# The taps of a depthwise convolution moved from VectorE to ScalarE and POOL, in a fused two-block kernel

## The reference, cut to what matters

```
y_a = gdn_mixer(...)     # gated delta rule: per chunk a triangular matrix is inverted, then a state runs over chunks
y_b = dsa_mixer(...)     # indexed attention: keys by top-128 of index scores, then softmax over them
y_c = conv_mixer(ug, dw, dw_b, ln_g, ln_b)
x = x + concatenate([y_a, y_b, y_c]) @ w_out

def conv_mixer(ug, dw, dw_b, ln_g, ln_b):
    u, gate = split(ug, 2)
    y = u * sigmoid(gate)
    y = causal_depthwise_conv(y, dw) + dw_b        # 31 taps, 256 channels
    y = layer_norm(y, ln_g, ln_b)                  # mean and variance over the 256 channels
    return silu(y)
```

## Time and profile before

| what | value |
|---|---|
| median of 3 runs | 1610.46 us (1610.21 to 1611.06) |
| profiled execution, its own time | 1610.98 us |
| its span, first to last instruction | 1609.2 us |
| granted TensorE clock | 0.996 of full |
| PE busy in the span | 98% |
| DVE busy in the span | 57% |
| ACT busy in the span | 43% |
| POOL busy in the span | 10%, all of it in the first fifth |

### The profile page before, as it was taken

One profiled execution on the slowest core, in us unless ns is written; L12 is line 12 of the kernel. 1 busy time (PEld: TensorE's weight loads), 2 busy tenths in 40 slices (PEclk: granted clock), 3 DMA queues, 4 the chain that ended last, 5 costly groups with the idle time before them and its releaser, 6 DMA issues.

```text
span 1609.2 us, 21520 instructions
## 1 busy us (share of the span) xinstructions
PE 1573.3 (98%) x7488; PEld 1305.9 (81%) x7488; DVE 918.1 (57%) x1322; ACT 685.1 (43%) x997; POOL 157.9 (10%) x97
## 2 busy tenths in 40 slices
PE   5999999999999999999999999999999999999997
PEld 5788798888788888888788888888888888888886
DVE  5469799765664324444477666666455544544332
ACT  5635554554653213433245455554224434443221
POOL 2435586200000000000000000000000000000000
PEclk9999999999999999999999999999999999999998
DMA  7422100122132232323233333333222323222332
GB/s 278 164 89 69 53 1 1 66 92 92 40 103 93 92 104 92 100 96 104 59 109 104 94 94 94 94 94 107 102 92 92 105 91 104 91 96 85 100 98 78
DMA packets 45665, 149.50 MB, mean 93 GB/s; under 512 B 4784, under 2 KB 5936, under 8 KB 45616
## 3 DMA queue, kind: packets, MB, share of 16 engines
q1 hardware_dynamic: 42240, 139.90, 27.2%
q10 hardware_dynamic: 3376, 8.95, 1.5%
HBM read 146.47 MB, written 2.10 MB: 92 GB/s over the span
## 4 chain that ended last, share of the span: by engine, by line
PE 90%; DVE 6%; ACT 2%; DMA 2%; issue 0%; ACTq 0%; DVEq 0%; SPq 0%
PE acc L628 84%; DVE c_acc L2109 1%; DVE tok L2249 1%; DMA x<-xT 1%; DVE d_score_a L2252 1%; DVE d_score_b L2252 1%; DMA raw<-panels_a 0%; PE acc L1114 0%; PE acc L1135 0%; DVE g_x L2235 0%; DVE w_lo L1977 0%; PE acc L801 0%; PE acc L703 0%; ACT w_hi L1378 0%; PE acc L939 0%
## 5 line engine op out<-in xcount | busy, mean ns | idle before, releaser
L628 PE MATMUL acc<-h_hi,w_hi 128*128 128x512 f32 x1248 | 491.5, 394 | 1.4 <-issue 0.8
L628 PE MATMUL acc<-h_lo,w_hi 128*128 128x512 f32 x1248 | 486.6, 390 | 0.0
L628 PE MATMUL acc<-h_hi,w_lo 128*128 128x512 f32 x1248 | 486.5, 390 | 0.0
L1985 DVE TENSOR_TENSOR w_lo<-raw,w_hi 128x1024 fp32r<-128x1024 f32 (+2 forms) x241 | 281.6, 1171 | 79.7 <-ACT w_hi L1385 57.6
L1385 ACT ACTIVATE w_hi<-raw 128x1024 fp32r<-128x1024 f32 (+2 forms) x241 | 242.0, 1008 | 175.5 <-PE acc L628 87.1
L628 PEld LDWEIGHTS acc<-h_hi,w_hi 128*128 128x128 f32 x1248 | 234.9, 188 | 52.4 <-issue 3.8
L628 PEld LDWEIGHTS acc<-h_hi,w_lo 128*128 128x128 f32 x1248 | 234.7, 188 | 49.1
L628 PEld LDWEIGHTS acc<-h_lo,w_hi 128*128 128x128 f32 x1248 | 234.8, 188 | 48.1 <-issue 1.0
L2390 DVE TENSOR_TENSOR x<-x,acc 128x512 f32 x32 | 22.0, 688 | 136.5 <-PE acc L628 136.0
L628 PE MATMUL acc<-u_hi,w_hi 128*128 128x512 f32 x256 | 99.6, 389 | 0.0
L628 PE MATMUL acc<-u_lo,w_hi 128*128 128x512 f32 x256 | 99.6, 389 | 0.0
(11 more groups left out here) (400 smaller groups left out, 2316.2 us busy)
## 6 DMA issues: line engine op xcount, KB each, us to landing
raw<-panels_a SPq DMA_DIRECT2D x112, 512.0 KB, 3.2
raw<-panels_b SPq DMA_DIRECT2D x68, 512.0 KB, 3.2
raw<-mix SPq DMA_DIRECT2D x48, 448.0 KB, 3.3
raw<-mix SPq DMA_DIRECT2D x16, 512.0 KB, 3.6
raw<-down SPq DMA_DIRECT2D x16, 384.0 KB, 3.1
raw<-down SPq DMA_DIRECT2D x16, 320.0 KB, 2.9
x<-xT ACTq DMA_DIRECT2D x4, 1024.0 KB, 9.8
x_rows<-xN ACTq DMA_DIRECT2D x2, 1024.0 KB, 9.6
```

The lines of the kernel that those rows point to most:

```text
L628: mm = e.matmul(out, w[:, w_at:w_at + wn], a, start=first and n == 0, stop=last and n == 2)
L1985: TTn(lo, raw, k.w_hi[:, ahead.slot(w)].bitcast(F32), ALU.subtract).then_inc(k.s_split_done, 1)
```

## The change

All 31 taps of tile 0 and the last 12 of tile 1 are now made by ScalarE and POOL: 43 parts in place of 31. One part lies in each of the 24 units, and the last seven are two to a pair in pairs 0 to 3; POOL has 24 adds in the units and nine behind. VectorE keeps the 19 taps ahead of the inverse. Selection is no longer two rounds in three units but four steps in every unit, 96 in all as before. The mean moves from behind unit 21 to pair 5, its subtraction from behind unit 22 to pair 6, the sums of squares from pair 1 to pairs 10 and 11 (in bank 0), the variance to pair 12. outputs(4), the first to use bank 3 again, waits for the subtraction. POOL's squares and its split of panels 32 to 34 stand behind all adds, thus behind pair 6. The turned probabilities d_pt move from the memory of c_y to that of g_p.

```diff
--- before.py
+++ after.py
@@ -48,6 +48,8 @@
 DOWN_W = [(b - a) * P for a, b in zip(DOWN_CUTS, DOWN_CUTS[1:])]
 MIX_GATES = next(p for p in range(8) if 34 <= MIX_CUTS[p + 1])
 CONV_TAPS = 31
+DVE_TAPS = 19
+CONV_PARTS = 2 * CONV_TAPS - DVE_TAPS
 PAD = 32
 
 REST, CKV, CQ, UG, Z = 0, 1, 2, 4, 8
@@ -121,7 +123,7 @@
     "xk_sq d_gates_tok beta_done sp_exp xk_std dec_exp k_root dk_raw d_std go_std aq_std ").split())}
 
 DVE_ONCE = {n: i + 1 for i, n in enumerate((
-    "sp_in xk_inv g_ready dec_copied br qe dv_done d_inv dk_done c_dve c_bias go_bias go_inv "
+    "sp_in xk_inv g_ready dec_copied br qe dv_done d_inv dk_done c_bias go_bias go_inv "
     "aq_inv ").split())}
 
 
@@ -199,6 +201,7 @@
     k.sq, sq_end = sb("sq", 2 * T)
     k.g_sq, _ = sb("g_sq", 2 * T, at=sq_end - 2 * T * 4)
     k.g_p, _ = sb("g_p", 2 * T, at=sq_end - 2 * T * 4)
+    k.d_pt, _ = sb("d_pt", 2 * T, at=sq_end - 2 * T * 4)
     k.tok, _ = sb("tok", NTOK)
     top[0] += (128 - top[0]) % 512
     h0 = top[0]
@@ -224,7 +227,6 @@
     k.d_q, a = sb("d_q", 2 * T, at=a)
     k.d_k, a = sb("d_k", T, at=a)
     k.d_score_b, a = sb("d_score_b", T, at=a)
-    k.d_pt, _ = sb("d_pt", 2 * T, at=a)
     k.c_y, a = sb("c_y", 2 * (PAD + T), at=a)
     k.c_acc, a = sb("c_acc", 2 * T, at=a)
     k.c_t, _ = sb("c_t", 2 * T, at=a)
@@ -341,6 +343,7 @@
     k.s_c_y = sem("c_y")
     k.s_c_part = sem("c_part")
     k.s_c_pool = sem("c_pool")
+    k.s_c_dve = sem("c_dve")
     k.s_c_cent = sem("c_cent")
     k.s_c_sq = sem("c_sq")
     k.s_c_norm = sem("c_norm")
@@ -567,15 +570,16 @@
         TTn(til(k.g_b, u % 4).rearrange("p (c i) -> p c i", c=TT), til(k.g_at, h).rearrange("p (c i) -> p c i", c=TT),
             mask, ALU.mult).then_inc(k.s_bt_done, 1)
 
-    acc = k.c_acc[:, 0:T]
-
     def conv_add(n):
 
         e.wait_ge(k.s_c_part, n + 1)
         if n:
             e.wait_ge(k.s_c_pool, n)
-        other = acc if n else col(k, "dw_b").broadcast_to([P, T])
-        TTn(acc, til(k.c_m, n % 2), other, ALU.add).then_inc(k.s_c_pool, 1)
+        if n == CONV_TAPS:
+            e.wait_ge(k.s_c_dve, DVE_TAPS)
+        sums = til(k.c_acc, int(n >= CONV_TAPS))
+        other = sums if n else col(k, "dw_b").broadcast_to([P, T])
+        TTn(sums, til(k.c_m, n % 2), other, ALU.add).then_inc(k.s_c_pool, 1)
 
     first = FRONT_AT["q0"] + SPLIT + 1
     early = 8 + len(FRONT_AT)
@@ -585,8 +589,9 @@
             conv_add(p - first)
     for u in range(UNITS):
         masked(u)
-        if early - first + u < CONV_TAPS:
-            conv_add(early - first + u)
+        conv_add(early - first + u)
+    for n in range(early - first + UNITS, CONV_PARTS):
+        conv_add(n)
     for j in range(2):
         e.wait_ge(k.s_c_cent, j + 1)
         TTn(til(k.c_t, j), til(k.c_acc, j), til(k.c_acc, j), ALU.mult).then_inc(k.s_c_sq, 1)
@@ -912,23 +917,25 @@
         mm.then_inc(k.s_xp_mm, 1)
         if 1 <= u <= UNITS - HEADS:
             turn_inverse(u - 1)
-        if u == UNITS - 3:
-
-            e.wait_ge(k.s_c_pool, CONV_TAPS)
-            e.wait_ge(k.s_dve_once, DVE_ONCE["c_dve"])
-            for j in range(2):
-                mm = e.matmul(k.ps[3][:], ones, til(k.c_acc, j), start=j == 0, stop=j == 1)
-            mm.then_inc(k.s_pe_once, 1)
     left("z3")
     left("kt3")
-    def centred_squares():
+
+    def conv_mean():
+
+        e.wait_ge(k.s_c_pool, CONV_PARTS)
+        for j in range(2):
+            mm = e.matmul(k.ps[3][:], ones, til(k.c_acc, j), start=j == 0, stop=j == 1)
+        mm.then_inc(k.s_pe_once, 1)
+
+    def centred_squares(t0):
 
         e.wait_ge(k.s_c_sq, 2)
-        for t in range(TT):
+        for t in range(t0, t0 + 2):
             for j in range(2):
-                mm = e.matmul(k.ps[3][:, t:t + 1], til(k.c_t, j)[:, t * P:(t + 1) * P], ones[:, 0:1],
+                mm = e.matmul(k.ps[0][:, t:t + 1], til(k.c_t, j)[:, t * P:(t + 1) * P], ones[:, 0:1],
                               start=j == 0, stop=j == 1)
-        mm.then_inc(k.s_pe_once, 1)
+        if t0:
+            mm.then_inc(k.s_pe_once, 1)
 
     def logits(u):
 
@@ -957,7 +964,7 @@
         qt, h = u // HEADS, u % HEADS
         e.wait_ge(k.s_pt_copied, u + 1)
         if h == 0 and qt == 1:
-            e.wait_ge(k.s_dve_once, DVE_ONCE["c_bias"])
+            e.wait_ge(k.s_c_cent, 2)
         if h == 0 and qt >= 2:
             e.wait_ge(k.s_att_lo, qt - 1)
         for t in range(qt + 1):
@@ -1042,8 +1049,8 @@
             old_state_outputs(c)
         if i + 1 < PAIRS:
             logits(i + 1)
-        if i == 1:
-            centred_squares()
+        if i == 5:
+            conv_mean()
         if i >= 3:
             outputs(i - 3)
         if i >= 8 and i % HEADS == 0:
@@ -1052,6 +1059,8 @@
             if c == 0:
                 e.wait_ge(k.s_wt_done, HEADS)
             state_and_outputs(c)
+        if i in (10, 11):
+            centred_squares(2 * (i - 10))
         if 1 <= i <= PAIRS:
             turn(i - 1)
         if PAIRS - 1 <= i <= PAIRS + 1:
@@ -1492,8 +1501,12 @@
             e.wait_ge(k.s_c_y, 1)
         if n >= 2:
             e.wait_ge(k.s_c_pool, n - 1)
-        y = k.c_y[:, PAD - n:PAD - n + T]
-        A(til(k.c_m, n % 2), y, ACT.Copy, scale=col(k, "dw", CONV_TAPS - 1 - n)).then_inc(k.s_c_part, 1)
+        if n == CONV_TAPS:
+            e.wait_ge(k.s_c_y, 2)
+        j, lag = (0, n) if n < CONV_TAPS else (1, DVE_TAPS + n - CONV_TAPS)
+        y = k.c_y[:, j * (PAD + T) + PAD - lag:j * (PAD + T) + PAD - lag + T]
+        A(til(k.c_m, n % 2), y, ACT.Copy,
+          scale=col(k, "dw", j * CONV_TAPS + CONV_TAPS - 1 - lag)).then_inc(k.s_c_part, 1)
         parts.step()
 
     leave("rest", til(k.proj, REST))
@@ -1647,8 +1660,7 @@
         if u >= 2:
             e.wait_ge(k.s_xp_mm, u - 1)
         A(k.g_p[:, (u % 2) * T:(u % 2) * T + T // 2], k.ps[u % 2][:, 0:T // 2], ACT.Copy).then_inc(k.s_p_copied, 1)
-        if parts.at() < CONV_TAPS:
-            conv_part()
+        conv_part()
         if FILL[u][2] == KT:
             leave(FILL[u][0], til(k.proj, Z + int(FILL[u][0][1])), ACT.Silu)
         if u in TURNS:
@@ -1705,6 +1717,9 @@
         if i >= 2:
             turned(i - 2)
         exps(i)
+        for _ in range(2):
+            if parts.at() < CONV_PARTS:
+                conv_part()
         if i >= 8 and i % HEADS == 0:
             attended(i // HEADS - 2)
         if i % BEAT == 2 and i // BEAT < TT:
@@ -2107,11 +2122,8 @@
                 ins = TS(out, y, w, col(k, "dw_b", 1), ALU.mult, ALU.add)
             else:
                 ins = STT(out=out, in0=y, scalar=w, in1=out, op0=ALU.mult, op1=ALU.add)
-            if t == 0:
-                ins.then_inc(k.s_dve_once, 1)
-            else:
-                chain(ins)
-            taps.step()
+            ins.then_inc(k.s_c_dve, 1)
+            e.wait_ge(k.s_c_dve, taps.step())
 
     conv_taps(2)
     conv("q0", 0)
@@ -2224,7 +2236,7 @@
 
     found, replaced = [0] * TT, [0] * TT
     for u in range(UNITS):
-        h, last, rounds = u % HEADS, u >= UNITS - HEADS, u % 3 < 2
+        h, last = u % HEADS, u >= UNITS - HEADS
         e.wait_ge(k.s_xp_mm, u + 1)
         if last:
             own = til(k.g_xt, h)[0:64, :].rearrange("p (c t) -> p c t", c=TT)[:, :, 64:P]
@@ -2233,21 +2245,14 @@
             lev = 1 + u // HEADS
             own, part = halves(til(k.g_x, h), lev)[:, 0], packed(k.ps[2 + u % 2][:, 0:T // 2], lev)
         TTn(own, own, part, ALU.subtract).then_inc(k.s_x_done, 1)
-        if not rounds and taps.at() < CONV_TAPS:
-            conv_taps(2)
-        if u == UNITS - 2:
-            e.wait_ge(k.s_pe_once, PE_ONCE["c_mean"])
-            for j in range(2):
-                mixed = til(k.c_acc, j)
-                STT(out=mixed, in0=k.ps[3][:], scalar=-1.0 / 256, in1=mixed, op0=ALU.mult,
-                    op1=ALU.add).then_inc(k.s_c_cent, 1)
-        if rounds:
-
-            for qt in range(1, TT):
-                if u:
+        for n in range(4 * u, 4 * u + 4):
+
+            qt = 1 + n % 3
+            if n % 6 < 3:
+                if n >= 6:
                     e.wait_ge(k.s_dve_chain, replaced[qt])
                 found[qt] = link(e.max(tok(TOK_M8 + 8 * qt - 8, 8), scores[qt]))
-            for qt in range(1, TT):
+            else:
                 e.wait_ge(k.s_dve_chain, found[qt])
                 replaced[qt] = link(e.match_replace(scores[qt], tok(TOK_M8 + 8 * qt - 8, 8), scores[qt], TAKEN))
     e.wait_ge(k.s_xp_mm, UNITS)
@@ -2332,9 +2337,15 @@
             for qt in range(1, TT):
                 ins = TS(scores[qt], scores[qt], TAKEN, MASKED, ALU.not_equal, ALU.mult)
             chain(ins)
-        if i == 3:
+        if i == 6:
+            e.wait_ge(k.s_pe_once, PE_ONCE["c_mean"])
+            for j in range(2):
+                mixed = til(k.c_acc, j)
+                STT(out=mixed, in0=k.ps[3][:], scalar=-1.0 / 256, in1=mixed, op0=ALU.mult,
+                    op1=ALU.add).then_inc(k.s_c_cent, 1)
+        if i == BEAT * TT:
```

(2 more changed lines are left out.)

## The result

The changed kernel takes 1614.62 us at the median of 13 runs (1611.84 to 1615.53), the one before 1610.83 in 13 runs beside it (1610.08 to 1612.68): a ratio of 1.002, 95% interval 1.0013 to 1.0028. The forecast was 1610.9 with a range up to 1613.8, so the time lies 0.8 us above the range. The direction was forecast as "no change".

What follows compares the result with a forecast made beforehand. VectorE was taken to bound the inverse, TensorE only 0.4 us a unit behind; in the attention no engine is full. Terms -3.6 - 1.8 - 1.3 + 3.5 + 1.6 + 0.3 + 1.7 = +0.4 gave 1610.9 us, range 1607.5 to 1613.8.

Steps and rivals of the forecast that it cites:

- Step 4: Pairs 0 to 3: seven more ScalarE parts held to the pace of POOL's adds delay the squares; cost 3.5 us.
- lockstep rival: Pairs 0 to 3: adds of 1.74 us instead of 1.27 hold up the attention; 1613.1 to 1613.9 us, chance 0.14.
- Step 1: Inverse: VectorE's load per unit falls, TensorE becomes the bound at 2.88 us a unit; gain 3.6 us.
- step 2: Mean's four matmuls leave the inverse; gain 1.8 us, at least 1.2 if a wait of the last units replaces it.
- Step 3: Squared sums leave pair 1, where TensorE's next instruction needs g_vn; gain 1.3 us of 1.71.
- Step 5: Mean in pair 5 adds TensorE work ahead of new_values(2), covered only by a 0.24 us wait; cost 1.6 us.
- Step 6: Centring in pair 6: outputs(4) waits for two VectorE subtractions, mostly covered by other TensorE work; cost 0.3 us.
- Step 7: Squared sums in pairs 10 and 11, where the chain is TensorE alone; cost 1.7 us.
- the 0.7 named as the sign of a wrong step: Pairs 0 to 3: ScalarE idle over 0.7 us before a part would show the parts-and-adds step wrong.
- new_values(2) only 2 us earlier: Sign of a right forecast: in the attention, new_values(2) would start only 2 us earlier than in the kernel before.
- step 8: POOL's squares and panel splits, moved behind the centring, end at 314, before TensorE needs them at 327.21; no cost.

Runs made afterwards that it cites:

- e5: The changed kernel itself, measured again in a later series beside the kernel before: 1613.14 us, ratio 1.0014.
- e8: e4's kernel with the 16 matmuls of the squared sums moved from pair 1 into TensorE's wait in pair 3: 1609.17 us, ratio 0.9988.
- e4: The kernel before with only the inverse changed: four selection steps a unit, ten late taps kept on VectorE, all 33 parts in the units: 1607.50 us, ratio 0.9978.
- e3: The kernel before with five extra unused squares on ScalarE ahead of the square of pair 2, lengthening TensorE's wait: 1615.85 us, ratio 1.0031.
- e6: e3's kernel with four extra unused matmuls on TensorE in the lengthened wait: 1613.16 us, ratio 1.0015.
- e1: The changed kernel with four extra unused 512-column matmuls on TensorE in its wait for ScalarE's copy g_o: 1610.41 us, ratio 0.9999.
- e9: The changed kernel with e1's four matmuls, and selection in whole rounds as in the kernel before: 1611.53 us, ratio 1.0002.
- e10: The changed kernel with e1's four matmuls, and squared sums in pairs 10 and 11 over the first channel tile only: 1610.56 us, ratio 0.9998.
- e2: The changed kernel with ScalarE's two parts at the end of each pair, behind the square and the copy g_o: 1610.22 us, ratio 0.9991.
- e11: e8's kernel with one extra unused 512-column matmul behind the moved sums: 1607.79 us, ratio 0.998.
- e7: e2's kernel with two extra unused matmuls in TensorE's wait for g_o: 1609.60 us, ratio 0.9992.
- e12: e4's kernel with one extra 512-column matmul in TensorE's wait in pair 3: 1607.26 us, ratio 0.9977.

## Why the prediction was wrong, step by step

The failed step is 4. Its mechanism and the length of the delay were right; its price was not, for the wait that it puts on TensorE was priced as time alone, and the sum has no term for the clock: 1.6 us in the trace of the changed kernel and 2.1 in e5's, from L1005 to L1014. No rival had it: the lockstep rival lengthens adds to 1.74 us, but in the chain above they take 1.28 to 1.43. Each interval below is taken within one trace, so the earlier start is in none of them; the measured column is after less before:

| step | forecast | measured | from |
|---|---|---|---|
| 1 inverse | -3.6 | -3.1 | 57.83 against 60.94 |
| 2 mean out | -1.8 | -1.4 | twentieth product to L1041: 11.37 against 12.80 |
| 3 sums out | -1.3 | -1.1 | L1041 to L1014: 5.83 against 6.94 |
| 4 parts and adds | +3.5 | +3.1 | L1014 to L1005: 9.47 against 6.42 |
| the clock | none | +1.6 | L1005 to L1014: 3.87 against 2.31 |
| 5 mean in pair 5 | +1.6 | +1.8 | second L1014 to new values: 4.59 against 2.78 |
| 6 centring | +0.3 | 0.0 | new values to the next L1005: 11.23 against 11.20 |
| 7 sums | +1.7 | +1.7 | that L1005 to the projection: 22.88 against 21.16 |
| sum | +0.4 | +2.5 | |

- **Step 1.** The bound changed hands as forecast: between 204 and 264 TensorE is busy 59.09 us and VectorE 46.98 (59.61 before), and the first starts are 2.92 and 2.88 apart. The 0.5 us missing lie in the later units: from the eleventh product on, six starts are 2.97 or 2.98 apart.
- **Steps 2 and 3.** Behind the twentieth product another waited 0.91 us for ScalarE's copy (before, the longest wait there was 0.25), which is the lower bound that step 2 named. Step 3's gain arrived at L1014, but e8 shows that it is worth nothing by itself where TensorE then waits for ScalarE (on e4's kernel L1001 starts no sooner for it): there, a part of the +3.1 in the table only takes it back.
- **Step 4.** The first exponential starts at 277.93 (forecast 277.7), the first part follows it, and the square starts at 285.43, forecast 285.4. Part of that hit is luck: steps 1 and 2 gave 0.9 less than forecast, and the trace's head start of 0.6 made up for most of it. The waits in ScalarE's timeline (start us, us, ..., idle before and releaser):

```profile
280.56 0.72 ACT L1508 ACTIVATE c_m<-c_y,vec 128x512 f32<-128x512 f32 x1 [0.53 <-POOL c_acc L582]
281.99 0.72 ACT L1508 ACTIVATE c_m<-c_y,vec 128x512 f32<-128x512 f32 x1 [0.70 <-POOL c_acc L582]
...
284.80 0.72 ACT L1508 ACTIVATE c_m<-c_y,vec 128x512 f32<-128x512 f32 x1 [0.69 <-POOL c_acc L582]
285.43 0.58 ACT L1729 ACTIVATE g_x<-acc 128x512 f32<-128x512 f32 x1
```

 None is over 0.70, just inside the 0.7 named as the sign of a wrong step. This time it was VectorE's third score instruction that waited out an add, on line 2338:

```profile
L2338 DVE TENSOR_SCALAR d_score_b<-d_score_b x1: 1494/1494/1494, 279.3 to 279.3; 128x512 f32<-128x512 f32 x1
```

 1.49 us instead of 0.41. That fits the exclusive lock on the shared port pair that the forecast took from the Trainium skill ("SBUF — State Buffer", section "SBUF: two separate sides"), but the add beside it was longer by 0.15 only (1.43 against 1.28), where the forecast had 0.76 for POOL. Three gaps of 0.13 us from one add to the next, which it had not counted, made up 0.4 of the rest.
- **The clock.** In the profile of before the clock is 1.00 behind the wait of 2.16 us, so no row of this stretch asks for the term. But step 4's own cost made that wait longer by up to 3.5 us (it grew by 2.2, to 4.34), and what the clock does then belonged among the rivals: e3 and e6 put it at 2.5 us on the kernel before. Both traces of the changed kernel lose the clock behind the wait (after, e5), all three with the wait filled keep it (e1, e9, e10). The forecast's sign "new_values(2) only 2 us earlier" failed with it: they start at 295.01, before at 294.85. The Trainium skill has it in "TensorE: Matmul & The Clock Gate", section "HAM oscillation — how this bites in real kernels": where TensorE waits long enough between bursts, the next burst starts at half the clock. The traces of after, e3 and e5 agree, with 0.50 to 0.60 behind waits of 4.3 to 5.3 us; e2 shows the same behind 2.06. But the clock also fell where TensorE had hardly waited (0.40 us in e11) or not at all (below).
- **Step 5** cost 1.8 in its own interval, and POOL's last add was done (287.7 + 1.28 = 289.0) long before the mean at 292.90: no wait there, as forecast. **Step 6** was hidden: outputs(4) waited 0.29 us for the subtraction, and the wait for g_o in pair 6 (0.24 before, none now) took it up. **Step 7** stands by e10, **step 8** too: POOL's splits end 15 us before the projection.

The remaining gap is in the medians: the traces of after and e5 lose 1.7 and 2.2 us to e1, the medians 4.2 (of different series) and 2.7. The mean granted clock of each execution is on record and fits that. It was 0.993 to 0.995 in the 13 executions of the first series (0.9941 on average), lowest in the longest, and 0.995 to 0.998 in e1's (0.9969). Of the 33 executions of the kernel before beside e9 to e12, the eleven at 0.995 have a median of 1612.39 us and the six at 0.997 one of 1609.45, so 0.001 of mean clock goes with some 1.5 us. The 0.0028 between the changed kernel and e1 are then 4.1 us, an estimate from these numbers, which is the whole gap. In which stretch the slower executions lost it isn't shown, since none of them was profiled.

One place where it can be lost is the same in all 14 traces and lies ahead of the change. In the kernel before, TensorE's timeline and a stretch behind it:

```profile
66.12 1.84 PE L738 MATMUL acc<-const,mem 128*128 128x1 f32 x16
67.82 1.03 PE L703 MATMUL acc<-const,g_sq 128*128 128x1 f32 x8
```

```profile
70.00:72.00 2.00, 2.00 (x6) 1.54 (x6) 0.00 (x0) 1.89 (x4) 1.15 (x2) 0.50 0.00 0
```

TensorE never waits here (it is busy 4.00 of every 4 us from 56 to 84), and yet behind these 24 matmuls of one column the clock is 0.50, and a product of 512 columns starts every 0.43 us instead of 0.23. It costs 1.6 us: from L703 to its next group 8.09, against 6.49 in e7 and e10. Twelve of the 14 traces lose the clock here, e7 and e10 keep it with the same instructions. Behind 24 matmuls of two columns near 178 us three of the 14 lose it (e6, e9, e10), for 1.6 us again. So e9's profiled execution is 3.6 us longer than e1's, with the same stretch. This is a source of the spread of every kernel here, and it shows that the same code can lose the clock in one execution and keep it in another.

## What to carry to other kernels

When a change makes TensorE's wait in an otherwise full stretch longer, price it twice: its length, and 1.5 to 2.5 us more behind it, which is what the half clock cost here. Look at the granted clock right behind each wait of TensorE before judging the engines' order; a few 512-column matmuls nobody needs, in the wait, brought that time back in e1 and e6, and the clock was kept in six of the seven kernels that had them (not in e11). The time that an engine idles in a stretch (TensorE 4.5 us in the attention) is no cover for added work unless it falls where the work is put: here none of 3.5 us was hidden.

## What the runs showed of the hardware

- The clock fell to 1.2 GHz inside a stretch in which TensorE is busy nine tenths of the time, in six traces (after, e2, e3, e5, e8, e11). It can fall during the wait (0.62 in 283 to 287 in e5, 0.86 in 289 to 291 in e3) or at its end (after), and in e3 and e5, where it fell during the wait, it was down for longest (e3: 0.50 from 291 to 297).
- The length of the wait doesn't decide alone: kept behind 2.16 us (before), 1.70 (e4) and 1.87 (e6), lost behind 2.06 (e2), 1.37 (e8) and 0.40 (e11).
- Sixteen matmuls of one column with their weight loads are recorded as 1.84 us of a busy TensorE; in both kernels that had them in the wait (e8, e11) the clock fell, in the two like them without (e4, e12) it did not, one trace of each. Behind 24 of them near 66 us it fell in 12 of 14 traces without any wait. A kernel with the same number of wide matmuls in their place was not run, and what exactly decides stays open.
- The execution time of one and the same kernel goes with its mean granted clock: 1612.39 us at 0.995 against 1609.45 at 0.997 in the kernel before.
